# Hybrid decoder layer on one core: high products first in every unit, and a fifth place for up units

## Chip, core and metric

One core of a Trainium2 chip runs the whole layer. The time is the device time of one execution in microseconds; each kernel is run several times and the median counts. The profile shows one execution. Matrix products run on TensorE (PE), weight loads into it are shown as PEld; VectorE is DVE, ScalarE is ACT, GpSimd is POOL, and SyncE (SP) issues the loads and stores.

## The reference, cut to what matters

1024 prompt tokens and 8 x 4 sample tokens of width 1024 pass one layer in float32:

```python
h = rmsnorm(x, g_mix); proj = h @ w_in           # to a gated DeltaNet and a Conformer convolution
o, s_new = gated_delta_rule(q, k, v, g, beta, s0)
x = x + concat([o, cv]) @ w_out
h = rmsnorm(x, g_mlp)
x = x + square(relu(h @ w_up)) @ w_down          # 1024 -> 4096 -> 1024
gate = sigmoid(rmsnorm(x, g_ple) @ w_ple_gate)
x = x + (p_emb @ w_ple) * gate                   # and a last rmsnorm
```

Besides the two outputs the new DeltaNet states and convolution histories are returned.

## The kernel before, in words

**Products in three parts.** TensorE works in a rounded float32 form. To keep float32 accuracy every operand is split in a high part (the value rounded) and a remainder, and a product is the sum of three: high weights by high rows, high weights by low rows, low weights by high rows. The weights of a unit are loaded into `w_raw` (L732, SP), ScalarE rounds them to `w_hi` (`split_hi`, L968), VectorE subtracts to `w_lo` (`split_lo`, L1692), in place of `w_raw`. There are three slots of weights, so the load of a unit waits until the unit three places before it has been multiplied.

**Units.** `plan()` lists 258 jobs, called units here. A unit is one block of 128 columns of one weight matrix by all tokens of a segment. Segment 0 has 512 tokens (one piece of 512 columns), segment 1 has 544 (two pieces of 256 and 288). Most units have `kts` = 8 blocks of depth, hence 24 products in a piece; a down unit of segment 0 has 4 (12 products), a ple unit 2. The order of kinds is: input projection of both segments (ab, qkv, gb, ga, z), then `rest(0)`, then `rest(1)`; `rest` has 8 out units, then groups of up units and 8 down units each, then 8 pairs of gate and ple. `GROUPS` gives the up units in a group: 8 groups of 4 in segment 0, 4 groups of 8 in segment 1. A down unit sums over the up units of its group and is added to `xT`.

**Slots.** Every unit has two slots of the loop that all engines run in the same order. TensorE multiplies a unit in one go per slot (`multiply`, products at L1345): the two pieces of segment 1, or the two halves of the depth in segment 0. `TIMES` counts the slots in units of work, and `schedule()` puts side work (the samples, the chunked scan, the inverses, the norms, and the taps of the depthwise convolution on VectorE, L2046) at times of that count; the taps are spread so as to load VectorE evenly.

**Evictions.** A result lies in one of two PSUM banks, used in turn; the eviction frees it. For a unit of segment 0 it comes in the first slot of the next unit, and in VectorE's queue it stands right ahead of the `split_lo` of the unit after that one. Out and down units are added to `xT` (`take_rows`, L1730). An up unit goes: VectorE relu and scale (L1721), ScalarE square (L1045), ScalarE copy to `u_hi` (L1047), VectorE subtraction to `u_lo` (`finish_up`, L1808). After out units and after the last down units ScalarE writes `hh_hi` (L1036, L1057) and VectorE `hh_lo` (L1796); the operands of the out units are `op_hi` and `op_lo` (L2086).

**What a unit waits for.** At its first product TensorE waits for `w_lo` and for its bank. The first unit of each kind also waits, at the first product of each depth block, for the low rows of that block (`ready`). The products run block by block:

```python
for i in ks:
    ready(job, c, i)
    for n, (wt, x) in enumerate(((w_hi, rhs[0]), (w_hi, rhs[1]), (w_lo, rhs[0]))):
```

Of the kernel before, what the change touches and what calls it, by code (L numbers as in the profile page):

```python
# [7 lines left out]
F32 = mybir.dt.float32  # L8
# [5 lines left out]
P = 128  # L14
# [32 lines left out]
GROUPS = [[4] * 8, [8] * 4]  # L47

# [101 lines left out]
def schedule():  # L150
# [203 lines left out]
    for k in range(KT):  # L354
        put(done + 3 + 3 * k, "xr", 1, k)
# [88 lines left out]
def build(nc, a, o):  # L444
    ctx = ExitStack()
    with ctx:
# [3 lines left out]
        WR = CR + 18176 + 4 * H * HT  # L450
# [10 lines left out]
        def at(region, name, shape, dt=F32, off=None):  # L461

            if off is None:
# [28 lines left out]
        rate = at(CR, "rate", [P, H, HT])  # L492
        rn = at(CR, "rn", [P, NT + 1, 2 * H])
# [29 lines left out]
        uu = [[at(M0, f"u0_{n}", [P, GROUPS[0][0], TS[0]], F32R, off=49152 + 8192 * i) for i, n in enumerate(("hi", "lo"))],  # L523
              [at(MX, f"u1_{n}", [P, GROUPS[1][0], TS[1]], F32R, off=29696 + 17408 * i) for i, n in enumerate(("hi", "lo"))]]
# [36 lines left out]
        rateT = at(MX, "rateT", [H * HT, P])  # L561
        rates = at(MX, "rates", [P, C])
# [3 lines left out]
        Tbd = at(MX, "Tbd", [P, 2, H, P], off=12288)  # L566
# [152 lines left out]
        def _(sp):  # L719
# [243 lines left out]
        def _(act):  # L963
# [349 lines left out]
        def _(pe):  # L1313
            def ready(job, c, i):
# [3 lines left out]
                if job.kind == "ab" and i == 0:  # L1318
                    for done_rows in (x_hi, x_lo):
                        pe.wait_ge(done_rows, NT + 1 if s else HT)  # L1320
                elif job.kind == "out" and job.i == 0:
                    pe.wait_ge(op_lo, s * KT + i + 1)
                elif job.kind == "up" and job.i == 0:
                    pe.wait_ge(h_lo, lo_count(s, 0, k, c))
                elif job.kind == "gate" and job.i == 0:
                    pe.wait_ge(h_lo, lo_count(s, 1, k, c))
                elif job.kind == "down" and job.i == 0:
                    pe.wait_ge(u_lo, u_count(s, job.first + k, c))
                elif job.kind == "ple" and job.i == 0 and i == 0:
                    pe.wait_ge(b6, SIX[("pe", TILES[s][-1])] + 1)  # L1330

            def multiply(job, c, ks):
                s, m = job.s, job.m
                rhs = {"out": op, "up": hh, "gate": hh, "down": uu, "ple": pp}.get(job.kind, hm)[s]
# [5 lines left out]
                for i in ks:  # L1340
                    ready(job, c, i)
                    k = ORDER[i] if job.kind == "out" else i
                    end = i == job.kts - 1
                    for n, (wt, x) in enumerate(((w_hi, rhs[0]), (w_hi, rhs[1]), (w_lo, rhs[0]))):
                        last = nc.tensor.matmul(dst, wt[job.slot][:, k, 0:m], x[:, k, lo:hi], start=(i == 0 and n == 0),  # L1345
                                                stop=(end and n == 2))
                if ks[-1] == job.kts - 1:
# [325 lines left out]
            for h in range(SLOTS):  # L1673
                if h // 2 < len(JOBS):
                    job = JOBS[h // 2]
                    if job.n == 2:
                        multiply(job, h % 2, range(job.kts))
                    else:
                        multiply(job, 0, range(job.kts // 2) if h % 2 == 0 else range(job.kts // 2, job.kts))
# [6 lines left out]
        def _(dve):  # L1686
# [117 lines left out]
            def finish_up(job, c):  # L1804
                lo, hi = PIECES[job.s][c]
                i = job.i % GROUPS[job.s][0]
                dve.wait_ge(u_hi, u_count(job.s, job.i, c))
                nc.vector.tensor_tensor(uu[job.s][1][:, i, lo:hi], sg[:, lo:hi], uu[job.s][0][:, i, lo:hi].bitcast(F32),  # L1808
# [351 lines left out]
```

## Time and profile before

| | |
|---|---|
| Runs | 1666.9, 1668.41, 1675.49 us, median 1668.41 |
| The profiled execution's own time | 1667.82 us |
| Its span, first to last instruction | 1666.0 us |
| TensorE matmuls under way | 1535.3 us, 92% of the span |
| VectorE busy | 983.2 us, 59% |
| ScalarE busy | 710.6 us, 43% |
| GpSimd busy | 61.9 us, 4% |
| Mean granted TensorE clock | 0.967 |

The trace is read from TensorE outward: how long it stands idle, which instruction of which engine ended that idle time, and what that instruction itself had waited for or was queued behind. Matmuls are pipelined: their starts are recorded and their ends are modelled, so the start-to-start distance is the rate. A granted clock of 1.00 is the 2.4 GHz level, 0.50 the 1.2 GHz level.

### The profile page before, as it was taken

What the parts mean: (1) busy time and instruction counts of PE and PEld (TensorE: products, weight loads), DVE (VectorE), ACT (ScalarE), POOL (GpSimd) and SP (SyncE); (2) the same over time, 40 slices, a digit from 0 to 9 for tenths busy, and PEclk for the clock granted to TensorE, in tenths of its full rate; (3) what the DMA queues carried; (4) which work ended last, traced back from release to release, by engine and by line L of the source; (5) the groups of instructions that cost most, each with busy time, mean ns of one, the idle gap of its engine ahead of it and who ended that gap; (6) DMA issues with size and microseconds to landing.
All of it is one profiled execution on the core that took longest, in us unless ns stands there. A gap on an engine that the chain in (4) does not pass through costs nothing.

```text
span 1666.0 us, 27343 instructions
## 1 busy us (share of the span) xinstructions
PE 1535.3 (92%) x11338; PEld 1342.7 (81%) x11338; DVE 983.2 (59%) x1709; ACT 710.6 (43%) x1088; POOL 61.9 (4%) x84
## 2 busy tenths in 40 slices
PE   4898978999989899789999999899999999999987
PEld 2786777999877676566777877679899999999987
DVE  3664999787564747678964554656443434434553
ACT  5546534534546323435322244545541423224455
POOL 0000100000000030010000100000000000000000
PEclk9999989999899989999998999999999999999999
DMA  6254435233123333332331213423332323333322
GB/s 192 77 143 117 110 106 153 76 88 84 40 68 104 65 82 98 106 94 73 97 81 48 74 39 93 129 79 117 95 89 87 90 86 89 89 89 88 93 67 86
DMA packets 282512, 153.42 MB, mean 92 GB/s; under 512 B 37428, under 2 KB 273132, under 8 KB 282381
## 3 DMA queue, kind: packets, MB, share of 16 engines
q1 hardware_dynamic: 281367, 150.39, 31.6%
q8 instruction: 90, 1.47, 0.4%
q10 hardware_dynamic: 1022, 1.28, 0.3%
q14 instruction: 33, 0.27, 0.1%
HBM read 135.06 MB, written 17.00 MB: 91 GB/s over the span
## 4 chain that ended last, share of the span: by engine, by line
PE 70%; DVE 15%; ACT 7%; issue 4%; DMA 3%; ACTq 0%; POOL 0%; SPq 0%; DVEq 0%
PE ps L1345 58%; DVE of L2046 3%; PE ps L1488 2%; DVE w_lo L1692 2%; PE ps L1522 2%; PE ps L1516 2%; DVE Xp L1961 1%; DVE prod L1960 1%; DMA qt<-qkv_dram 1%; PE ps L1478 1%; ACT L972 1%; DVE yb L1721 1%; DVE u_lo L1808 1%; PE ps L1569 1%; DMA Lp<-lt_dram 1%
## 5 line engine op out<-in xcount | busy, mean ns | idle before, releaser
L1345 PE MATMUL ps<-hh_hi,w_hi 128*128 128x256 f32 (+1 forms) x960 | 317.9, 331 | 15.4 <-DVE w_lo L1692 9.6
L968 ACT ACTIVATE w_hi<-w_raw 128x1024 fp32r<-128x1024 f32 (+3 forms) x258 | 231.2, 899 | 214.9 <-DMA w_raw<-in_w_down 107.8
L1692 DVE TENSOR_TENSOR w_lo<-w_raw,w_hi 128x1024 fp32r<-128x1024 f32 (+3 forms) x258 | 266.5, 1033 | 86.9 <-ACT w_hi L968 86.0
L1345 PE MATMUL ps<-hh_lo,w_hi 128*128 128x256 f32 (+1 forms) x960 | 312.4, 325 | 0.0
L1345 PE MATMUL ps<-hh_hi,w_lo 128*128 128x256 f32 (+1 forms) x960 | 311.6, 325 | 0.0
L1345 PE MATMUL ps<-u_hi,w_hi 128*128 128x512 f32 (+2 forms) x768 | 256.5, 334 | 25.0 <-DVE u_lo L1808 18.7
L1345 PE MATMUL ps<-u_lo,w_hi 128*128 128x512 f32 (+2 forms) x768 | 249.3, 325 | 0.0
L1345 PE MATMUL ps<-u_hi,w_lo 128*128 128x512 f32 (+2 forms) x768 | 249.1, 324 | 0.0
L1345 PE MATMUL ps<-hm_hi,w_hi 128*128 128x512 f32 (+5 forms) x600 | 208.8, 348 | 13.4 <-DVE w_lo L1692 4.8
L1345 PEld LDWEIGHTS ps<-hh_hi,w_hi 128*128 128x128 f32 x960 | 182.8, 190 | 38.3 <-DVE w_lo L1692 18.7
L1345 PE MATMUL ps<-hm_lo,w_hi 128*128 128x512 f32 (+5 forms) x600 | 199.5, 332 | 0.0
L1345 PE MATMUL ps<-hm_hi,w_lo 128*128 128x512 f32 (+5 forms) x600 | 198.5, 331 | 0.0
L1345 PEld LDWEIGHTS ps<-hh_hi,w_lo 128*128 128x128 f32 x960 | 182.4, 190 | 14.0
L1345 PEld LDWEIGHTS ps<-hh_lo,w_hi 128*128 128x128 f32 x960 | 183.0, 191 | 12.9 <-issue 0.7
L1345 PEld LDWEIGHTS ps<-u_hi,w_hi 128*128 128x128 f32 x768 | 145.5, 189 | 44.4 <-DVE u_lo L1808 22.1
L2046 DVE SCALAR_TENSOR_TENSOR of<-gl,wdw,of 128x512 f32<-128x512 f32 x240 | 172.9, 763 | 1.1
L1730 DVE TENSOR_TENSOR xT<-xT,ps 128x512 f32<-128x512 f32 (+2 forms) x152 | 84.0, 553 | 131.4 <-PE ps L1345 131.0
L1345 PEld LDWEIGHTS ps<-u_hi,w_lo 128*128 128x128 f32 x768 | 145.3, 189 | 11.3
L1345 PEld LDWEIGHTS ps<-u_lo,w_hi 128*128 128x128 f32 x768 | 145.8, 190 | 10.2 <-issue 1.1
L1045 ACT ACTIVATE yb<-yb 128x256 f32<-128x256 f32 (+1 forms) x96 | 47.8, 498 | 230.6 <-DVE yb L1721 230.6
L1345 PEld LDWEIGHTS ps<-hm_hi,w_hi 128*128 128x128 f32 (+1 forms) x600 | 116.3, 194 | 29.2 <-issue 13.3
L1345 PEld LDWEIGHTS ps<-hm_lo,w_hi 128*128 128x128 f32 (+1 forms) x600 | 116.2, 194 | 11.6 <-issue 3.0
(286 smaller groups left out, 2035.5 us busy)
## 6 DMA issues: line engine op xcount, KB each, us to landing
w_raw<-in_w_up SPq DMA_DIRECT2D x64, 512.0 KB, 3.9
w_raw<-in_w_in SPq DMA_DIRECT2D x48, 512.0 KB, 4.1
w_raw<-in_w_down SPq DMA_DIRECT2D x64, 256.0 KB, 2.7
w_raw<-in_w_down SPq DMA_DIRECT2D x32, 512.0 KB, 4.0
w_raw<-in_w_out SPq DMA_DIRECT2D x16, 512.0 KB, 4.1
w_raw<-in_w_ple_gate SPq DMA_DIRECT2D x16, 512.0 KB, 4.1
qt<-qkv_dram SPq DMA_DIRECT2D x8, 768.0 KB, 5.9
xin<-in_x_prompt SPq DMA_DIRECT2D x8, 512.0 KB, 6.3
```

Of the source, the lines that this page charges most:

```text
L968: nc.scalar.activation(w_hi[job.slot][:, 0:job.kts, 0:job.m], w_raw[job.slot][:, 0:job.kts, 0:job.m], ACT.Copy).then_inc(w_hid, 1)
L972: ac.step(nc.scalar.activation(dst, src, ACT.Ln, **kw))
L1045: nc.scalar.activation(sg[:, lo:hi], yb[i % 2][:, lo:hi], ACT.Square).then_inc(u_sq, 1)
L1345: last = nc.tensor.matmul(dst, wt[job.slot][:, k, 0:m], x[:, k, lo:hi], start=(i == 0 and n == 0), stop=(end and n == 2))
L1478: last = nc.tensor.matmul(ps[:, 7, h * HD:(h + 1) * HD], T, Vb[:, t % HT, h * HD:(h + 1) * HD], start=True, stop=True)
L1488: last = nc.tensor.matmul(ps[r, bank + par, q * HD:(q + 1) * HD], src[rows, q, r], S[rows, q, :], start=(first or q == 0), stop=first, ski ...
L1516: last = nc.tensor.matmul(ps[par * HD:(par + 1) * HD, 2, q * HD:(q + 1) * HD], Kd[r, t % HT, h * HD:(h + 1) * HD], Vn[r, h * HD:(h + 1) * ...
L1522: last = nc.tensor.matmul(ps[r, 4 + par, q * HD:(q + 1) * HD], LQ[r, t % HT, par * PR + q, 0, :], Vn[r, h * HD:(h + 1) * HD], start=False, ...
L1569: last = nc.tensor.matmul(ps[rows, 2, q * 2 * NS:(q + 1) * 2 * NS].rearrange("p (w t) -> p w t", w=2)[:, :, cols], S0[rows, q, b, :], WQ[r ...
L1692: nc.vector.tensor_tensor(w_lo[job.slot][:, 0:job.kts, 0:job.m], w_raw[job.slot][:, 0:job.kts, 0:job.m], w_hi[job.slot][:, 0:job.kts, 0:jo ...
L1730: nc.vector.tensor_tensor(rows, rows, src, ALU.add).then_inc(freed(job, c), 1)
L2046: ins = nc.vector.scalar_tensor_tensor(out=rows, in0=gl[:, p, k:k + HALF], scalar=w, in1=rows, op0=ALU.mult, op1=ALU.add)
```

## The change

Three things change. Products of a unit are ordered high by high for all depth blocks first, then the two kinds with a remainder: high weights by low rows before low weights by high rows, in the first unit of a kind the other way round. TensorE waits for `w_hi` at the first product and for `w_lo` at the first product that uses it; the row waits are for high and low rows apart. In segment 0 a fifth place holds one more up unit: the first up unit of the next group runs ahead of the down units of this one (the last group has 3 up units left). ScalarE writes the square to `u_hi` first and then the plain square, in place of a square and a copy of it. Beside this some scratch moves to other addresses, and the loads of input rows 5 to 7 of segment 1 come after the last down unit of segment 0, since the fifth place lies in their memory.

```diff
+PLACES = [5, 8]
...
-        first = 0
+        first = made = 0
         for n in GROUPS[s]:
-            jobs.extend(Job("up", s, first + i) for i in range(n))
+            ready = min(first + PLACES[s], FF // P)
+            jobs.extend(Job("up", s, i) for i in range(made, ready))
             jobs.extend(Job("down", s, m, first, kts=n, last=first + n == FF // P) for m in range(KT))
-            first += n
+            first, made = first + n, ready
...
-        put(done + 3 + 3 * k, "xr", 1, k)
+        put(max(done + 3 + 3 * k, half("gate", 0, 0) + k - 4 if k > 4 else 0), "xr", 1, k)
...
+        u_fifth = [at(M0, "u0_hi4", [P, TS[0]], F32R, off=65536), at(MX, "u0_lo4", [P, TS[0]], F32R, off=12288)]
...
+        def u_rows(s, x, i):
+
+            k = i % PLACES[s]
+            return uu[s][x][:, k, :] if k < uu[s][x].shape[1] else u_fifth[x][:, :]
...
+                    if k > 4:
+                        sp.wait_ge(mm, last_unit("down", 0, KT - 1))
...
                 gone(act, job, c)
+                nc.scalar.activation(u_rows(s, 0, i)[:, lo:hi], yb[i % 2][:, lo:hi], ACT.Square).then_inc(u_hi, 1)
                 if i:
                     act.wait_ge(u_lo, u_count(s, i - 1, c))
                 nc.scalar.activation(sg[:, lo:hi], yb[i % 2][:, lo:hi], ACT.Square).then_inc(u_sq, 1)
-                act.wait_ge(u_sq, u_count(s, i, c))
-                nc.scalar.activation(uu[s][0][:, i % GROUPS[s][0], lo:hi], sg[:, lo:hi], ACT.Copy).then_inc(u_hi, 1)
...
+            def products(job):
...
+                first = (1, 0) if job.i == 0 else (0, 1)
+                rest = [(i, w, 1 - w) for w in first for i in range(job.kts)]
+                return [(i, 0, 0) for i in range(job.kts)] + rest
...
-                    for done_rows in (x_hi, x_lo):
-                        pe.wait_ge(done_rows, NT + 1 if s else HT)
+                    pe.wait_ge(x_lo if low else x_hi, NT + 1 if s else HT)
                 elif job.kind == "out" and job.i == 0:
-                    pe.wait_ge(op_lo, s * KT + i + 1)
+                    pe.wait_ge(op_lo if low else op_hi, s * KT + i + 1)
                 elif job.kind == "up" and job.i == 0:
-                    pe.wait_ge(h_lo, lo_count(s, 0, k, c))
+                    pe.wait_ge(h_lo if low else h_hi, lo_count(s, 0, k, c))
                 elif job.kind == "gate" and job.i == 0:
-                    pe.wait_ge(h_lo, lo_count(s, 1, k, c))
+                    pe.wait_ge(h_lo if low else h_hi, lo_count(s, 1, k, c))
                 elif job.kind == "down" and job.i == 0:
-                    pe.wait_ge(u_lo, u_count(s, job.first + k, c))
+                    pe.wait_ge(u_lo if low else u_hi, u_count(s, job.first + k, c))
...
-                if ks[0] == 0:
-                    pe.wait_ge(w_lod, job.j + 1)
+                remainder = min(n for n, (_, w, _) in enumerate(todo) if w)
+                if first == 0:
+                    pe.wait_ge(w_hid, job.j + 1)
                     wait(pe, pf[u % 2], u // 2)
...
+                for n in range(first, end):
+                    i, w, x = todo[n]
+                    if n == max(first, remainder):
+                        pe.wait_ge(w_lod, job.j + 1)
+                    if not w:
+                        ready(job, c, i, x)
                     k = ORDER[i] if job.kind == "out" else i
...
+                    last = nc.tensor.matmul(dst, weights[w][:, k, 0:m], rows[:, lo:hi], start=n == 0, stop=n == size - 1)
...
-                dve.wait_ge(u_hi, u_count(job.s, job.i, c))
+                dve.wait_ge(u_sq, u_count(job.s, job.i, c))
```

## Rows read from the trace of the kernel before

**Rows 1.** The page: busy time of engines, and the chain that ended last.
```profile
PE 1535.3 (92%) x11338; PEld 1342.7 (81%) x11338; DVE 983.2 (59%) x1709; ACT 710.6 (43%) x1088; POOL 61.9 (4%) x84
...
PE 70%; DVE 15%; ACT 7%; issue 4%; DMA 3%; ACTq 0%; POOL 0%; SPq 0%; DVEq 0%
```

**Rows 2.** Waits of TensorE: who for whom, us in total, times, longest us.
```profile
PE ps L1345 <- DVE w_lo L1692: 21.9, 22, 4.8
PE ps L1345 <- DVE u_lo L1808: 18.7, 8, 7.2
```

**Rows 3.** Timeline of TensorE (start us, us, instruction, idle before), first down unit, 702.
```profile
702.74 0.39 PE L1345 MATMUL ps<-u_hi,w_hi 128*128 128x512 f32 x1
702.97 0.39 PE L1345 MATMUL ps<-u_lo,w_hi 128*128 128x512 f32 x1
703.19 0.40 PE L1345 MATMUL ps<-u_hi,w_lo 128*128 128x512 f32 x1
...
710.82 0.80 PE L1345 MATMUL ps<-u_hi,w_hi 128*128 128x512 f32 x1 [7.23 <-DVE u_lo L1808]
```

**Rows 4.** Timeline of VectorE in the same stretch: eviction of up unit 11, its remainder.
```profile
708.04 0.68 DVE L1721 SCALAR_TENSOR_TENSOR yb<-ps,rs 128x512 f32<-128x512 f32 x1
...
710.08 0.69 DVE L1808 TENSOR_TENSOR u_lo<-yb,u_hi 128x512 fp32r<-128x512 f32 x1 [0.76 <-ACT u_hi L1047]
```

**Rows 5.** Waits of TensorE for u_lo, from 745 to 845, 845 to 975, 1015 to 1045.
```profile
PE ps L1345 <- DVE u_lo L1808: 3.6, 2, 2.2
...
PE ps L1345 <- DVE u_lo L1808: 3.3, 1, 3.3
...
PE ps L1345 <- DVE u_lo L1808: 0.8, 1, 0.8
```

**Rows 6.** Windows: stretch, length, busy PE PEld DVE ACT POOL, PEclk, DMA share, GB/s.
```profile
891.00:902.00 11.00, 11.00 (x74) 8.63 (x73) 1.73 (x3) 0.63 (x1) 0.61 (x1) 0.53 0.08 24
```

**Rows 7.** Waits of TensorE for w_lo, 1045 to 1066, to 1078, 1086 to 1128, to 1136.
```profile
PE ps L1345 <- DVE w_lo L1692: 2.3, 3, 1.4
...
PE ps L1345 <- DVE w_lo L1692: 3.5, 1, 3.5
...
PE ps L1345 <- DVE w_lo L1692: 3.3, 6, 0.6
...
PE ps L1345 <- DVE w_lo L1692: 1.2, 1, 1.2
```

**Rows 8.** Timeline of VectorE at 655: eviction, then the split of the next.
```profile
654.77 0.68 DVE L1730 TENSOR_TENSOR xT<-xT,ps 128x512 f32<-128x512 f32 x1
655.37 0.69 DVE L1692 TENSOR_TENSOR w_lo<-w_raw,w_hi 128x512 fp32r<-128x512 f32 x1
```

**Rows 9.** Timeline of all engines, last down units and gate unit 0.
```profile
1061.87 0.42 DVE L2091 TENSOR_TENSOR pp_lo<-ps,pp_hi 128x256 fp32r<-128x256 f32 x1 [1.04 <-ACT pp_hi L1254]
...
1065.34 0.50 PE L1345 MATMUL ps<-hh_hi,w_hi 128*128 128x512 f32 x1 [1.44 <-DVE w_lo L1692]
...
1067.25 0.72 ACT L1057 ACTIVATE hh_hi<-xT,vec 128x512 fp32r<-128x512 f32 x1 [1.45 <-DVE xT L1730]
```

**Rows 10.** Timeline of ScalarE and TensorE ahead of the first unit.
```profile
28.91 1.02 ACT L1091 ACTIVATE hm_hi<-ps 128x1024 fp32r<-128x1024 f32 x1 [1.31 <-PE ps L1375]
...
31.34 0.59 PE L1345 MATMUL ps<-hm_hi,w_hi 128*16 128x512 f32 x1 [2.46 <-DVE hm_lo L1855]
```

**Rows 11.** Timeline of TensorE in output unit 0.
```profile
484.66 0.51 PE L1345 MATMUL ps<-op_hi,w_hi 128*128 128x512 f32 x1 [3.10 <-DVE op_lo L2086]
```

**Rows 12.** Timeline of TensorE at z unit 2 of segment 1.
```profile
241.57 0.55 PE L1345 MATMUL ps<-hm_hi,w_hi 128*128 128x256 f32 x1 [4.67 <-ACT yb L1014]
```

**Rows 13.** Windows: VectorE alone (busy, PEclk, DMA), then all engines as in rows 6.
```profile
794.00:832.00 38.00, 35.14 (x67) 1.00 0.30 91
...
531.00:1134.00 603.00, 554.72 (x3621) 433.45 (x3619) 382.41 (x624) 234.07 (x340) 40.51 (x47) 0.96 0.30 84
...
1086.00:1128.00 42.00, 38.66 (x163) 29.82 (x163) 26.00 (x39) 20.35 (x32) 0.00 (x0) 1.00 0.31 92
```

More of the change, by code:

```diff
@@ L449, in build @@
         CR = base
-        WR = CR + 18176 + 4 * H * HT
+        WR = CR + 18176 + 4 * H * HT + 4 * C
         TR = WR + 3 * 8192
@@ L492, in build @@
         rate = at(CR, "rate", [P, H, HT])
+        rates = at(CR, "rates", [P, C])
         rn = at(CR, "rn", [P, NT + 1, 2 * H])
@@ L522, in build @@
                for i, n in enumerate(("hi", "lo"))] for s in range(2)]
-        uu = [[at(M0, f"u0_{n}", [P, GROUPS[0][0], TS[0]], F32R, off=49152 + 8192 * i) for i, n in enumerate(("hi", "lo"))],
-              [at(MX, f"u1_{n}", [P, GROUPS[1][0], TS[1]], F32R, off=29696 + 17408 * i) for i, n in enumerate(("hi", "lo"))]]
+        uu = [[at(M0, f"u0_{n}", [P, 4, TS[0]], F32R, off=49152 + 8192 * i) for i, n in enumerate(("hi", "lo"))],
+              [at(MX, f"u1_{n}", [P, PLACES[1], TS[1]], F32R, off=29696 + 17408 * i) for i, n in enumerate(("hi", "lo"))]]
+        u_fifth = [at(M0, "u0_hi4", [P, TS[0]], F32R, off=65536), at(MX, "u0_lo4", [P, TS[0]], F32R, off=12288)]
         op = [[at(MX, f"op{s}_{n}", [P, KT, TS[s]], F32R, off=32768 + 17408 * i)
@@ L560, in build @@
         trk = [at(MX, f"trk{n}", [P, H, C]) for n in range(2)]
-        rateT = at(MX, "rateT", [H * HT, P])
-        rates = at(MX, "rates", [P, C])
+        rateT = at(MX, "rateT", [H * HT, P], off=22528)
         cur[MX] = 30720
@@ L565, in build @@
         assert cur[MX] == 32768
-        Tbd = at(MX, "Tbd", [P, 2, H, P], off=12288)
+        Tbd = at(MX, "Tbd", [P, 2, H, P], off=14336)
         Lp = at(MX, "Lp", [P, C * C])
@@ L1313, in _, with ready @@
         def _(pe):
-            def ready(job, c, i):
+            def products(job):
+                first = (1, 0) if job.i == 0 else (0, 1)
+                rest = [(i, w, 1 - w) for w in first for i in range(job.kts)]
+                return [(i, 0, 0) for i in range(job.kts)] + rest
+            def ready(job, c, i, low):
                 s, n = job.s, len(PIECES[job.s])
@@ L1325, in ready @@
                 elif job.kind == "gate" and job.i == 0:
-                    pe.wait_ge(h_lo, lo_count(s, 1, k, c))
+                    pe.wait_ge(h_lo if low else h_hi, lo_count(s, 1, k, c))
                 elif job.kind == "down" and job.i == 0:
-                    pe.wait_ge(u_lo, u_count(s, job.first + k, c))
-                elif job.kind == "ple" and job.i == 0 and i == 0:
+                    pe.wait_ge(u_lo if low else u_hi, u_count(s, job.first + k, c))
+                elif job.kind == "ple" and job.i == 0 and i == 0 and not low:
@@ L1330, in ready, with multiply @@
                     pe.wait_ge(b6, SIX[("pe", TILES[s][-1])] + 1)
-            def multiply(job, c, ks):
+            def multiply(job, c, half=None):
                 s, m = job.s, job.m
-                rhs = {"out": op, "up": hh, "gate": hh, "down": uu, "ple": pp}.get(job.kind, hm)[s]
+                rhs = {"out": op, "up": hh, "gate": hh, "ple": pp}.get(job.kind, hm)[s]
+                weights = (w_hi[job.slot], w_lo[job.slot])
                 dst, lo, hi = out_of(job, c)
                 u = job.u + c
-                if ks[0] == 0:
-                    pe.wait_ge(w_lod, job.j + 1)
-                    wait(pe, pf[u % 2], u // 2)
-                for i in ks:
-                    ready(job, c, i)
-                    k = ORDER[i] if job.kind == "out" else i
[L1343 to L1347, printed above, removed]
+                todo = products(job)
+                size = len(todo)
+                first, end = {None: (0, size), 0: (0, size // 2), 1: (size // 2, size)}[half]
+                remainder = min(n for n, (_, w, _) in enumerate(todo) if w)
+                if first == 0:
+                    pe.wait_ge(w_hid, job.j + 1)
+                    wait(pe, pf[u % 2], u // 2)
+                for n in range(first, end):
[4 more added lines that the diff above has]
+                        ready(job, c, i, x)
+                    k = ORDER[i] if job.kind == "out" else i
+                    rows = u_rows(s, x, job.first + k) if job.kind == "down" else rhs[x][:, k, :]
+                    last = nc.tensor.matmul(dst, weights[w][:, k, 0:m], rows[:, lo:hi], start=n == 0, stop=n == size - 1)
+                if end == size:
@@ L1676, in _ @@
                     if job.n == 2:
-                        multiply(job, h % 2, range(job.kts))
+                        multiply(job, h % 2)
                     else:
-                        multiply(job, 0, range(job.kts // 2) if h % 2 == 0 else range(job.kts // 2, job.kts))
+                        multiply(job, 0, h % 2)
                 for stage in SIDE[h]:
```

3 lines of the change are left out of this document (1 added, 2 removed).

## Prediction

> **What bounds the kernel now.** I read the page first: TensorE has matmuls under way for 92% of the span, VectorE is busy for 59%, and the chain that ended last is 70% TensorE, 15% VectorE [rows 1]. So a microsecond that TensorE does not stand still is nearly a microsecond won, as long as VectorE's queue isn't what it then waits for. The second view is the waits of TensorE: the two largest at the product line L1345 are 22 waits for `w_lo` (21.9 us) and 8 for `u_lo` (18.7 us) [rows 2]. They are what this change aims at, 40.6 us, and the rest of the working asks of each what would be late next. The third view is the timeline around one wait. A product of 512 columns follows the last after 0.23 us, whether the weights stay (`u_hi,w_hi` to `u_lo,w_hi`) or change (to `w_lo`), and a product whose own wait is already met (702.74) starts as promptly. A wait costs its idle time and 0.17 us to start again: 703.19 to 710.82 is 7.63 us, of which 0.23 is the pitch and 7.23 the idle time [rows 3]. The first matmul behind a wait also lasts 0.50 us [rows 9], not 0.40 as at 703.19, and holds up the next by as much. So I count 0.28 us beside each wait's idle time.
>
> **Part 1, the fifth place.** It concerns units of segment 0 alone (segment 1 had 8 places for groups of 8). There each group ends with an up unit whose eviction is a chain: VectorE L1721, ScalarE L1045 and L1047, VectorE L1808, and the first down unit needs its `u_lo` at its tenth product, 2.1 us after it starts. With the next group's first up between (24 products, 5.5 us), that is due 5.5 us later. The waits of the first seven groups go: 18.7 less the last group's 0.8 (no up unit is left to put there) [rows 5] is 17.9, with 7 x 0.28 it is 19.9 us. One of them does not go whole. At 702 VectorE works off side work (a chunk's scaling) and empties up unit 11's bank only from 708.04 to 708.7 [rows 4]. There are two result banks used in turn, so the down unit behind the extra up unit (701.36 + 5.5 = 706.9) must wait for that bank: 1.9 us stay. **18.0 us.** In the last group the first down unit now needs `u_hi` at its fourth product, 0.7 us after it starts; the first ScalarE pass now writes `u_hi` itself, one pass earlier. I put that group at 0: about 1 us of wait for `u_hi` instead of 0.8 for `u_lo`.
>
> The two longest of these waits (7.2 and 3.3) had a second price: behind the 3.3 us wait TensorE ran at a granted clock of 0.53 from 891 to 902, which is the 1.2 GHz level for nearly all of it [rows 5, 6]. If all the work in those 11 us were twice as fast, 5.2 us would come back; if other gaps bring the level down anyway, nothing. I take **2.5 us** for both places together, about the middle, since small matmuls of side work fill much of that stretch.
>
> The extra unit moves two weight loads and their splits on SP, ScalarE and VectorE with it, in the same queues and in the same number. The side work (state scan, samples, inverses) is placed by time in units of work, so it keeps its time and gets another neighbour. I cost that at nothing.
>
> **Part 2, remainders last.** Every unit now waits for `w_hi` at its start and for `w_lo` only at its first product with it: 16 products later in an 8-deep unit (3.7 us), 8 later in a down unit of segment 0 (1.8 us), 8 later also in the first unit of each kind. All the idle times for `w_lo` but five are under 1.3 us, so the wait itself is gone. But in VectorE's queue the instruction just ahead of the split is the eviction that frees the bank the waiting unit writes: at 654.77 L1730, at 655.37 the split, both for the unit that starts at 656.11 [rows 8]. So the unit can start at most one split earlier (0.6 us in a down unit, 1.2 in a deep one) when VectorE has a backlog. By stretch:
> - Six waits at gate units of segment 0: 3.3 us idle [rows 7], each shorter than the 1.2 us split: whole, 3.3 + 6 x 0.28 = 5.0.
> - The first output unit of segment 1, 1.2 us [rows 7]: its pieces have 256 columns, so `w_lo` is due after 8 x 0.12 = 0.9 us: 1.0.
> - Ten waits in the up and down units: 21.9 - 4.8 - 2.3 - 3.5 - 3.3 - 1.2 = 6.8, with 2.8 for restarts 9.6; two of 1.5 and 1.6 us give one split each (less 1.7), one stands before side work that waits for GpSimd anyway (less 0.9): 7.0.
> - The 4.8 us wait of z unit 1 (segment 1) gives 0: 16 products could run early, but the unit behind it waits 4.7 us more for ScalarE's eviction, which VectorE's inverse work holds up [rows 12].
> - The last three of that kind ahead of the gates, 2.3 us, give 0. There the last down units run to a loop of 3.9 us between VectorE and ScalarE (L2091 idles 1.04 us in each round for ScalarE [rows 9]), and TensorE only gets ahead of it.
>
> Sum **13.0 us.**
>
> **What the new order costs.** A first unit of a kind now needs all its high rows after 7 products instead of its low rows after 21. For gate unit 0 the last `hh_hi` is written from 1067.25 to 1067.97 [rows 9]. TensorE stalls there, and 17 products are left: 1067.97 + 17 x 0.23 = 1071.9, where before the unit ended at 1071.0 (24 products from 1065.34). Everything to gate unit 1 then comes 0.9 later, except that this unit needn't wait for its 1.2 us split: **+0.3 us** is left of the 3.5 us wait [rows 7]. Up unit 0 pays the same way: **-0.4** (nothing to 0.9, the gate's value). Output unit 0 loses its 3.1 us wait for `op_lo` at the 19th product and finds another at the 23rd, with two products left instead of six at the low clock: **+1.2** [rows 11]. The very first unit waited 2.46 us for `hm_lo`; the matching `hm_hi` ends at 29.93, so it can start at 30.1 instead of 31.34: **+1.3** [rows 10].
>
> **Edits with no cost of their own.** ScalarE and VectorE have as many instructions as before, only the order of `u_hi` and the plain square turns round. Three loads of input rows move behind the last down unit; they are first needed in the output units of segment 1, some 60 us on. The waits added to TensorE are met ones elsewhere, at 0 [rows 3].
>
> **What is given back.** From 794 to 832 VectorE is busy 35.1 of 38 us [rows 13]. The changes of the stretch 745 to 845 (3.6 us for `u_lo` [rows 5] and about as much again) would load it to some 99%. I take off **2 us** (0 to 5).
>
> Sum: 18.0 + 2.5 + 13.0 + 0.3 - 0.4 + 1.2 + 1.3 - 2 = 33.9 us. The profiled execution took 1667.8 us, of which the span is 1666.0 and the rest lies around it unchanged, so 1633.9; the median of the runs is 0.6 above it: 1634.5.
>
> **A rule against the change.** At 702.74, 702.97 and 703.19 the pitch is 0.23 us whether or not the weights change, so their loads are hidden [rows 3]. The Trainium skill (TensorE: Matmul & The Clock Gate, Architectural detail) says that TensorE's queue pulls weight loads ahead of matmuls in flight. By that rule a wait amid a unit would stop this running ahead and cost a restart; the restart measured is 0.28 us, and it is paid only where the wait isn't met.
>
> **Rivals.**
> - **The banks and VectorE's queue take over.** With evictions in the same order, TensorE meets its bank where it met `w_lo` or `u_lo`. For it: rows 8 and 4. Against: the gates have 1.2 us of split between. Then Part 2's seven in the up and down units and half of Part 1's 18.0 go, and the clock's 2.5: 33.9 - 7.0 - 9.0 - 2.5 = 15.4 us won, 1652.
> - **The change doesn't do what it says**: `w_hi` and `u_hi` come as late as the remainders, because ScalarE (which waits for VectorE too) sets both. Only Part 1's short waits and the gates are won, 8 us or less: 1660 or above. Against: `w_lo` comes 0.6 to 1.2 us after `w_hi` by VectorE's own time alone.
> - **Slower: the clock.** Long waits become many short ones. Over 531 to 1134 the clock is 0.96 [rows 13]. If it fell to 0.84 there, a further 24% of 603 us would be at the low level and cost half of that, 72 us against 34 won: 1706. It decides at 34/(603 x 0.5) = 11% more time at the low level, a mean of 0.90. Against: from 1086 to 1128 six such waits leave it at 1.00 [rows 13]. The Trainium skill (same page, A second HAM failure mode) tells of a kernel whose clock swung through just such short pauses between groups; here no row shows it.
>
> **Chances.** Forecast (1624 to 1645) 0.68; banks and queue (to 1656) 0.2; doesn't do what it says 0.08, of which 0.02 just below 1660; slower 0.04. The range 1624 to 1654 leaves out the last two and the tail of the second. The bound of what can be told from no change is 0.5%, 8.3 us: faster 0.9, same 0.06, slower 0.04.
>
> **What would show it.** Waits of TensorE for `u_lo` fall from 8 to 1 or 2, those for `w_lo` to a few under 1 us; new waits for the evictions L1730 and L1721 sum to under 6 us; at gate unit 0 a new wait of about 2 us for `hh_hi` stands amid the unit; the clock from 885 to 905 is above 0.8. I am wrong if the waits for evictions sum to over 15 us, or if the side work's waits grow.

## Result: 9 us won of the 33 forecast

The changed kernel takes 1659.0 us (median of 9 runs, 1649.7 to 1661.5) against 1667.9 us: the ratio is 0.9934 (95% interval 0.9913 to 0.9954; the ratios in this document go by all runs of both kernels, not by the two medians). Forecast were 1634.5 us and a range of 1624 to 1654. The sign was right, the size was not: 8.9 us came of 33.4. The profiled execution took 1652.7 us, 15.2 under the one of before; why it looks better than the median is told below.

The page of the changed kernel, busy time and chain (compare [rows 1]):

```profile
PE 1534.3 (93%) x11338; PEld 1344.7 (81%) x11338; DVE 982.7 (60%) x1709; ACT 701.8 (43%) x1088; POOL 62.4 (4%) x84
...
PE 72%; DVE 12%; ACT 7%; issue 4%; DMA 3%; POOL 1%; ACTq 0%; SPq 0%; DVEq 0%; POOLq 0%
```

Below are the waits of TensorE from the first up unit of segment 0 to its last down unit, 528.9 to 1053.7, called the stretch from here on (who for whom, us in total, times, longest). L1372 is the product line, L1756 and L1747 are the evictions that were L1730 and L1721, L978 is `split_hi`:

```profile
PE ps L1458 <- DMA qt<-qkv_dram: 6.4, 1, 6.4
PE ps L1372 <- DVE xT L1756: 4.8, 3, 3.1
PE ps L1372 <- DVE yb L1747: 3.6, 3, 1.9
PE ps L1372 <- ACT w_hi L978: 3.0, 2, 2.5
PE ps L1637 <- ACT cn L1218: 2.2, 2, 1.2
...
PE ps L1372 <- ACT u_hi L1053: 0.8, 1, 0.8
```

Before, the same stretch (531 to 1065.4) had

```profile
PE ps L1345 <- DVE u_lo L1808: 18.7, 8, 7.2
PE ps L1345 <- DVE w_lo L1692: 9.1, 13, 1.6
```

Both are gone. In their place stand 13.6 us for banks, `w_hi` and a norm's `cn` (4.8 + 3.6 + 3.0 + 2.2) that were not there.

**What stood in TensorE's way.** VectorE around the longest new wait (start, us, instruction), and TensorE at its end:

```profile
651.01 0.69 DVE L1954 TENSOR_TENSOR Vb<-ps,beta 128x512 f32<-128x512 f32 x1
651.61 0.68 DVE L1954 TENSOR_TENSOR tk<-ps,egc 128x512 f32<-128x512 f32 x1
652.21 0.68 DVE L1954 TENSOR_TENSOR Kbe<-ps,scb 128x512 f32<-128x512 f32 x1
652.81 0.68 DVE L1954 TENSOR_TENSOR Kd<-ps,scb 128x512 f32<-128x512 f32 x1
653.41 0.68 DVE L1756 TENSOR_TENSOR xT<-xT,ps 128x512 f32<-128x512 f32 x1
...
654.23 1.94 PE L1372 MATMUL ps<-u_hi,w_hi 128*128 128x512 f32 x4 [3.10 <-DVE xT L1756]
```

This is the scaling of a chunk: ten instructions, and ahead of them a wait of 1.1 us for ScalarE that begins at 648.6. Until 653.41, 4.8 us in all, the eviction is queued behind. A down unit lasts 2.75 us (12 products at 0.229 us), so two banks can't cover it; an up unit lasts 5.5 us and can. ScalarE holds up `w_hi` in the same way at 777, with the inverse root of a norm (a logarithm and an exponential), two table loads among them (4.4 us from 773.14 to the end of `w_hi`):

```profile
773.14 1.28 ACT L1223 ACT_TABLE_LOAD   x1
774.44 0.69 ACT L1223 ACTIVATE cn<-ps,eps 128x512 f32<-128x512 f32 x1
775.14 1.28 ACT L1225 ACT_TABLE_LOAD   x1
776.44 0.63 ACT L1225 ACTIVATE cn<-cn 128x512 f32<-128x512 f32 x1
776.97 0.61 ACT L978 ACTIVATE w_hi<-w_raw 128x512 fp32r<-128x512 f32 x1
...
777.64 2.07 PE L1372 MATMUL ps<-u_hi,w_hi 128*128 128x512 f32 x4 [2.55 <-ACT w_hi L978]
```

### The profile page after: what moved, and what is told of

Same layout as the page of the kernel before. It is cut to its first block, busy times and chain, and to the rows that moved or that the text cites. A ratio compares the mean times of both kernels' runs of the same rounds, so it can differ in the third digit from the quotient of the medians.

```text
span 1650.9 us, 27248 instructions
## 1 busy us (share of the span) xinstructions
PE 1534.3 (93%) x11338; PEld 1344.7 (81%) x11338; DVE 982.7 (60%) x1709; ACT 701.8 (43%) x1088; POOL 62.4 (4%) x84
## 4 chain that ended last, share of the span: by engine, by line
PE 72%; DVE 12%; ACT 7%; issue 4%; DMA 3%; POOL 1%; ACTq 0%; SPq 0%; DVEq 0%; POOLq 0%
PE ps L1372 59%; PE ps L1514 3%; PE ps L1548 2%; DVE of L2071 2%; PE ps L1542 2%; DVE w_lo L1718 1%; DVE Xp L1986 1%; DMA qt<-qkv_dram 1%; DVE prod L1985 1%; PE ps L1504 1%; PE ps L1595 1%; ACT w_hi L978 1%; POOL VnM L952 1%; ACT L982 1%; DMA Lp<-lt_dram 1%
## 5 line engine op out<-in xcount | busy, mean ns | idle before, releaser
L978 ACT ACTIVATE w_hi<-w_raw 128x1024 fp32r<-128x1024 f32 (+3 forms) x258 | 231.7, 901 | 229.5 <-DMA w_raw<-in_w_down 114.2
L1372 PE MATMUL ps<-hh_hi,w_hi 128*128 128x256 f32 (+1 forms) x960 | 179.3, 329 | 11.6 <-DVE yb L1747 3.1
L1372 PE MATMUL ps<-hh_lo,w_hi 128*128 128x256 f32 (+1 forms) x960 | 178.9, 326 | 0.0
L1372 PE MATMUL ps<-hh_hi,w_lo 128*128 128x256 f32 (+1 forms) x960 | 173.3, 323 | 0.0
L1372 PEld LDWEIGHTS ps<-hh_hi,w_hi 128*128 128x128 f32 x960 | 145.9, 191 | 30.4 <-issue 11.1
L1372 PE MATMUL ps<-u_hi,w_hi 128*128 128x512 f32 (+2 forms) x768 | 154.8, 337 | 12.1 <-DVE xT L1756 4.8
L1756 DVE TENSOR_TENSOR xT<-xT,ps 128x512 f32<-128x512 f32 (+2 forms) x152 | 83.9, 552 | 129.0 <-PE ps L1372 128.7
L1372 PEld LDWEIGHTS ps<-hh_lo,w_hi 128*128 128x128 f32 x960 | 145.9, 190 | 14.5 <-issue 1.3
L1372 PEld LDWEIGHTS ps<-hh_hi,w_lo 128*128 128x128 f32 x960 | 145.6, 189 | 13.2
L1372 PE MATMUL ps<-u_lo,w_hi 128*128 128x512 f32 (+2 forms) x768 | 149.1, 328 | 0.0
L1372 PE MATMUL ps<-u_hi,w_lo 128*128 128x512 f32 (+2 forms) x768 | 144.8, 324 | 0.0
L1372 PEld LDWEIGHTS ps<-u_hi,w_hi 128*128 128x128 f32 x768 | 116.2, 192 | 29.3 <-issue 13.2
L1372 PE MATMUL ps<-hm_hi,w_hi 128*128 128x512 f32 (+5 forms) x600 | 121.8, 348 | 8.9 <-ACT yb L1024 6.6
L1372 PEld LDWEIGHTS ps<-u_lo,w_hi 128*128 128x128 f32 x768 | 118.1, 192 | 11.7 <-issue 0.2
L1372 PEld LDWEIGHTS ps<-u_hi,w_lo 128*128 128x128 f32 x768 | 117.1, 189 | 11.3
L1372 PEld LDWEIGHTS ps<-hm_hi,w_hi 128*128 128x128 f32 (+1 forms) x600 | 94.8, 196 | 27.1 <-issue 16.1
L1372 PE MATMUL ps<-hm_lo,w_hi 128*128 128x512 f32 (+5 forms) x600 | 114.1, 330 | 0.0
L1372 PE MATMUL ps<-hm_hi,w_lo 128*128 128x512 f32 (+5 forms) x600 | 111.1, 327 | 2.4 <-DVE w_lo L1718 2.4
L1747 DVE SCALAR_TENSOR_TENSOR yb<-ps,rs 128x256 f32<-128x256 f32 (+1 forms) x96 | 49.9, 521 | 101.1 <-PE ps L1372 87.1
```

The lines of the kernel that those rows point to most:

```text
L978: nc.scalar.activation(w_hi[job.slot][:, 0:job.kts, 0:job.m], w_raw[job.slot][:, 0:job.kts, 0:job.m], ACT.Copy).then_inc(w_hid, 1)
L1372: last = nc.tensor.matmul(dst, weights[w][:, k, 0:m], rows[:, lo:hi], start=n == 0, stop=n == size - 1)
L1747: nc.vector.scalar_tensor_tensor(out=yb[i % 2][:, lo:hi], in0=src, scalar=0.0, in1=rs[:, lo:hi], op0=ALU.max, op1=ALU.mult).then_inc(freed ...
L1756: nc.vector.tensor_tensor(rows, rows, src, ALU.add).then_inc(freed(job, c), 1)
```

## Where the time of the stretch goes

For the stretch I split TensorE's time, from start to start of its instructions, in four: idle time as the trace gives it, products at their pitch at 2.4 GHz (1536 times 0.229 us, 351.7 us, the same in all and not shown), what a product took beyond that, which is restart or the 1.2 GHz level ("over pitch"), and the time of the side work's matmuls ("side"). Worked out from the rows of each trace, us:

```
kernel (traces)            total   idle   over pitch   side
before                     534.3   40.3   29.9         112.3
fifth place alone, 1st     526.4   35.9   28.4         110.3
fifth place alone, 2nd     522.9   34.4   27.5         109.3
new order elsewhere (*)    530.3   34.4   32.7         111.5
new order here (*)         525.4   33.4   30.0         110.3
new order alone            535.4   38.1   35.3         110.3
both (the change), 1st     524.7   29.8   30.9         112.2
both, 2nd                  520.3   30.4   28.7         109.5
both, 3rd                  529.1   31.3   35.2         110.9
```

(*) The two halves of experiment 2, both with the fifth place.

The prediction has 25.1 us for this stretch (18.0 + 2.5 + 7.0 - 0.4 - 2): by its own terms some 18.4 us of idle time and 6.7 of restarts and clock. The three traces of the change have 9.6 us in the mean: 9.8 us less idle time, 1.7 us more over pitch, 1.4 us less side work. So a good half of the 15.5 us that are missing here (8.6) is idle time, new waits above all, and the rest is restarts and clock that didn't get less. Time over pitch varies between executions: "new order elsewhere" runs the same instructions in the stretch as "fifth place alone" and has 4 to 5 us more of it. Outside the stretch the prediction has 8.8 us and the three traces have 4.0 in the mean.

## Experiments

**1. Either part alone.** The fifth place with the old order of products and its waits, run twice:

```diff
-                rest = [(i, w, 1 - w) for w in first for i in range(job.kts)]
-                return [(i, 0, 0) for i in range(job.kts)] + rest
+                return [(i, w, x) for i in range(job.kts) for w, x in ((0, 0), (0, 1), (1, 0))]
...
+                    if n == 0:
+                        pe.wait_ge(w_lod, job.j + 1)
```

> The changed kernel with the old order of products (block by block, remainder weights waited for at the first product); the fifth place stays. The steps of the prediction: Part 1 brings 18.0 and the clock 2.5, less 2 for VectorE's load and 0.4 less for up unit 0 than the full change, so about 18 us under the kernel before (1650). Theory of the banks (down units are 2.75 us long, two banks cover one of them, and each block of side work that VectorE does ahead of an eviction now stops TensorE there): the waits for u_lo vanish, but waits for the evictions yb and xT of 5 to 9 us and the side work's own waits come in units 4 to 16 of the up units, and the gain is 2 to 8 us (1660 to 1666). Theory of the clock: the waits vanish and stay away, but the mean granted clock from up unit 0 to the last down unit falls by 0.02 or more.

Measured: 1660.7 us, ratio 0.9966 (0.995 to 0.9983), 12 runs; on another chip 1658.9, 0.9958 (0.9934 to 0.9981). The waits of the stretch:

```profile
PE ps L1370 <- DVE w_lo L1716: 16.5, 13, 3.1
...
PE ps L1635 <- ACT cn L1218: 2.2, 2, 1.2
...
PE ps L1370 <- DVE yb L1745: 1.0, 1, 1.0
PE ps L1370 <- DVE u_lo L1831: 0.8, 1, 0.8
```

The waits for `u_lo` fell by 17.9 us as forecast, and those for `w_lo` rose from 9.1 to 16.5. As I read it, the old wait for `u_lo` had given VectorE time to catch up; without it TensorE meets the same backlog one or two units later. My expectation had these waits under the names of evictions; they came as `w_lo`, the split right behind the eviction in the queue. The theory of the clock fails here: in the stretch the clock rose from 0.96 to 0.97 in both traces, and over whole runs its mean was 0.9669 (24 runs) against 0.9649 (72 runs of before).

The new order with four places:

```diff
-PLACES = [5, 8]
+PLACES = [4, 8]
```

> The changed kernel with four places for up units, so the order of units of the kernel before; only the order of products is new. The steps of the prediction: Part 2's 13.0 and 2.4 from the new order in the first units, 15.4 us under the kernel before (1652.5), of it 7.0 in up and down units of segment 0. Theory of the banks: the first units and the gates bring their 2.5 and 5, the up and down units next to nothing, so 6 to 9 us (1659 to 1662), with u_lo waits of 14 to 19 us as before, since the first down unit now needs u_lo two products earlier (its eighth product instead of its tenth). Theory of the clock: gain under 5 us, with a lower mean clock.

Measured: 1670.4 us, ratio 1.000 (0.9984 to 1.0015): nothing.

```profile
PE ps L1372 <- ACT u_hi L1053: 19.4, 8, 7.1
...
PE ps L1372 <- DVE xT L1756: 3.2, 2, 1.6
...
PE ps L1372 <- ACT w_hi L978: 0.7, 2, 0.5
```

The two longest `w_lo` waits, 1.6 and 1.5 us, are now waits of 1.6 and 1.5 us for the eviction ahead of the split. The split was 0.6 us of them, but TensorE also came that much earlier to its bank, since a short wait before was gone, and the eviction didn't: at the longer one it starts 10.70 us after the chunk's transposes in both kernels (644.07 to 654.77 before, 645.67 to 656.37 now). The waits for `u_lo` became waits for `u_hi`, since a first down unit needs its last high rows at the fourth product. The idle time of the stretch fell by 2.2 us, and 5.4 us more over pitch took it back. The mean clock was 0.9607 (12 runs).

**2. Which half of the new order pays.** With five places, the new order either everywhere but in the up and down units of segment 0, or in these alone, beside the kernels with none and all of it, on one chip:

```diff
+                if job.s == 0 and job.kind in ("up", "down"):
+                    return [(i, w, x) for i in range(job.kts) for w, x in ((0, 0), (0, 1), (1, 0))]
```

> Five places, the new order of products everywhere but in the up and down units of segment 0, which keep the old order and its waits. The forecast's terms for this part of the order: 5.0 at the gates, 1.0 and 0.3 at first units, 1.2 and 1.3 at output unit 0 and the first unit, 8.8 us under the kernel with five places and the old order (1660.7), so 1652. From the traces so far: gates 5.1, the rest next to nothing, so 1655 to 1656. If the new order lowers TensorE's clock and that is a matter of the order itself, the mean clock is under that of the old order (0.967) here too.

> The other half: five places, the new order in the up and down units of segment 0 alone. The forecast gives it 7.0 less 0.4 us, 1654. By the traces TensorE's waits in this part are 35.9 us with the old and 29.8 us with the new order, but what it gains lies in a part with slow-clock stretches: 2 to 6 us, 1655 to 1659.

> The kernel with five places and the old order once more, on the same chip as the two halves: 1660.7 before; 1659 to 1663, mean clock 0.966 to 0.968.

> The changed kernel once more beside its two halves. If the halves are independent, its gain over the old order with five places is the sum of theirs; 1656 to 1660, mean clock 0.963 to 0.965.

Measured: none of it 1658.9 us, 0.9958 (0.9934 to 0.9981); all but up and down units 1659.9, 0.9950 (0.9926 to 0.9975); these alone 1660.8, 0.9951 (0.9934 to 0.9968); all of it 1659.5, 0.9941 (0.9922 to 0.9960). Beside the fifth place the new order is worth 0.0017 of 1668, 3 us, inside the intervals (over 24 runs each the means are 1662.3 and 1658.2, the medians 1659.8 and 1659.2). Yet the gates' gain is in every trace: from gate unit 0 to output unit 0 of segment 1, 68.8 us before, 69.3 and 67.9 us with the fifth place and the old order, 64.2, 64.2 and 65.8 us with the new. In the stretch the new order has 4.7 us less idle time, and the stretch is no shorter: 524.7 us in the mean with either order. What goes with the loss is the clock. Its mean over the runs is 0.9669 (24 runs, old order), 0.9654 and 0.9664 with half of it, 0.9637 (24 runs) with all of it. Within the 24 runs of the changed kernel 0.01 of clock goes with 11 us, within the 24 of the old order with 13, so these 0.003 are some 4 us.

The traces show where. With the old order in the up and down units (three traces with the fifth place) the granted clock is 0.96 from 606 to 682 and 1.00 from 682 to 741; with the new order there (four traces) it is 0.91 to 0.93 and 0.97. The waits in front are alike: 3.1 us at 651 to 657 in all seven, then 1.8 us with the old order and 1.9 with the new at 711 to 716. From 705 to 725 the clock is 1.00 in the three and 0.91 in the four. So a wait of the same length is followed by the 1.2 GHz level with one order and not with the other.

**3. Is it the order itself that lowers the clock?** Four places, new order, all waits as before:

```diff
+                    if n == 0:
+                        pe.wait_ge(w_lod, job.j + 1)
+                    if not w and not x:
+                        ready(job, c, i, 0)
+                        ready(job, c, i, 1)
```

> Four places, the new order of products, but every wait where it was: for the remainder weights at a unit's first product, for both parts of the rows at the first product of each depth block. It asks what the order alone does to TensorE's clock: the new order with the new waits had a mean clock of 0.9607 over 12 runs against 0.9651 before, at 5 us per 0.0044. If the order of products lowers the clock, 0.960 to 0.962 again and 1672 to 1676, since nothing is won. If the places of the waits do, 0.965 and 1668 to 1671 (the u_lo waits of the down units come two to six products earlier, at no gain).

Measured: 1687.9 us, 1.0134 (1.0115 to 1.0152), clock 0.9614. I had the time wrong: with the low rows waited for in the first eight products, a first down unit needs `u_lo` at its fourth product instead of its tenth, and those waits grew by half (18.7 to 28.8 us).

```profile
PE ps L1372 <- DVE u_lo L1833: 28.8, 9, 7.7
```

So waits for high and low parts apart are what makes the new order bearable at all. The clock was as low as with the new waits, but the stretch had 12 us more idle time than before (51.8 against 40.3), so this decides nothing. **Why the new order goes with a lower clock stays open.**

**4. The same kernel again.**

> The changed kernel once more, word for word, for a second trace of it: its runs lie from 1649.7 to 1661.5, the one traced was 1652.67. If the spread is TensorE's clock, two traces whose times differ have the same waits and differ in the mean granted clock, in stretches at the 1.2 GHz level (a difference of 8 us needs 16 us more at that level); if it is DMA or queueing, the waits of TensorE differ. Median again 1659, 1656 to 1661.

Measured: 1658.0 us (6 runs), 0.9933 (0.9908 to 0.9957). Three traces of the changed kernel, span and clock:

```profile
core 0: 1650.9 us, clock 0.963
...
core 0: 1647.1 us, clock 0.968
...
core 0: 1659.1 us, clock 0.964
```

In the stretch their waits agree to 0.3 us for `xT`, `yb`, `u_hi` and `cn` and to 0.8 us for `w_hi`; the time over pitch is 30.9, 28.7 and 35.2 us. So the spread goes with the clock, as expected, though the mean over the span doesn't rank the first and third rightly. It also counts the first 31 us, where TensorE has matmuls under way for less than 9 us and the first trace has 0.92, the third 1.00. Which stretches fall to 1.2 GHz changes in part from run to run behind the same gaps: from 561 to 606 the three have 0.85, 0.92 and 0.86. The Trainium skill (TensorE: Matmul & The Clock Gate, What's actually happening) says that the moment of the clock's first rise varies between runs of one kernel, with where the start falls in the gate's own rhythm. The three traces show variation amid the kernel; where it comes from they don't show. The two first traces happened to be good ones: their mean gain is 17.0 us, the means of all runs differ by 10.4 (1668.6 over 81 runs and 1658.2 over 24).

**5. Load or blocks?** In both kernels the convolution taps of segment 1 work on 32 of 512 columns (the rest of those rows is left out):

```diff
+                    n = 32 if s else HALF
-                    ins = nc.vector.scalar_tensor_tensor(out=rows, in0=gl[:, p, k:k + HALF], ...
+                    ins = nc.vector.scalar_tensor_tensor(out=rows[:, 0:n], in0=gl[:, p, k:k + n], ...
```

> The kernel before with the taps of segment 1's depthwise convolution cut to 32 of 512 columns (all but the first tap of each part; the rest of these rows is left out of the computation), so VectorE's queue keeps its order and its waits and loses about 120 x 0.6 = 70 us of load between the first up unit and the last down unit. It is the base for the same cut in the changed kernel. If VectorE's load sets the waits for w_lo and u_lo, it is 8 us or more faster than the kernel before; if the chunk scaling and its chain do, the u_lo wait of 7.2 us at up unit 11 stays within 1.5 us and the gain is 2 to 6 us.

> The changed kernel with the same cut of taps. Theory of load (VectorE is too busy for the gain): against the same cut in the kernel before it gains 25 us or more, near the forecast 33.9, and its waits for the evictions xT and yb fall under 2 us. Theory of blocks (the four passes of a chunk's scaling and what they wait for stand ahead of an eviction in VectorE's queue, whatever the load around them): its waits for xT and yb keep over half of their 8.4 us and it gains 9 to 16 us against the same cut in the kernel before.

Measured: 1658.9 us, 0.9951 (0.9940 to 0.9963), and 1649.0 us, 0.9888 (0.9874 to 0.9903). VectorE is busy for 59 and 57 us less (983.2 to 924.1, 982.7 to 925.9; I had reckoned with 70). The change is worth 9.9 us with this load off, as much as with it. TensorE in the stretch, changed kernel with short taps:

```profile
PE ps L1372 <- DVE xT L1756: 4.3, 2, 3.4
...
PE ps L1372 <- DVE yb L1747: 0.5, 2, 0.3
```

The waits for `xT` behind the scaling stay, those for `yb` go: 4.8 of 8.4 us are left. So load is a part of these waits, but taking it off didn't bring the missing gain.

**6. The block itself.** The scaling cut in two, its last two wide passes behind the eviction, on top of the early loads of experiment 7:

```diff
+                passes = plan[:2] if HT <= t < NT else plan
...
         put(n, "sc", t)
+        if HT <= t < NT:
+            put(n + 1, "sd", t)
```

> The changed kernel with early qt loads, and the chunk scaling of segment 1 cut in two: the last two of its four wide passes (1.2 us at a pitch of 0.60 us) come one slot later, behind the eviction that the whole block stood ahead of. Theory of blocks: the two long waits for evictions in down units behind a scaling (3.1 us at up unit 8's group, 1.5 to 1.9 at up unit 12's) shrink by 1.2 us each, 2 to 4 us won (1642 to 1644). Rival (the block's start, set by the chain of squares and roots ahead of it, decides and not its length): waits and time as with the early loads alone, 1645.6 within 1.

Measured: 1644.3 us, 0.9864 (0.9848 to 0.9880), 1.3 us under its base, which can't be told from nothing. But the waits answer to the instruction: from 620 to 675 with the whole block, then cut,

```profile
PE ps L1372 <- DVE xT L1756: 3.3, 2, 3.1
```

```profile
PE ps L1374 <- DVE xT L1758: 2.1, 2, 1.9
```

The longest is shorter by 1.2 us, which is two passes at a pitch of 0.60 us. The one of 1.5 us in the next group (700 to 741) is now

```profile
PE ps L1374 <- DVE xT L1758: 0.3, 1, 0.3
```

That shows the block as the cause of these two waits, by dose. It shows nothing of the others: `yb` (3.8 us), `w_hi` (4.3 us) and `cn` (2.2 us) are as long with the cut as without; that blocks in the queues make them too is read from the timelines and not tested. (The stretch took 515.6 us against 518.9. In these two traces the last 530 us gave it back: 531.4 against 527.2, at a clock of 0.98 against 0.99.)

Then the chunk preparations moved between up units, in three versions:

```diff
-    for t in TILES[1][:HT]:
+    for t, up in zip(TILES[1][:HT], (9, 11, 13, 15)):
...
+        h = half("up", 0, up)
```

> The changed kernel with the preparation of segment 1's four chunks put at up units 9, 11, 13 and 15, so each chunk's scaling on VectorE stands between up units (5.5 us each) and none between down units (2.75 us each); the rest of the scan follows later by 11 units. Theory of blocks: the waits for the evictions xT and yb in segment 0's down units (8.4 us) go, with restarts 8 to 11 us under the changed kernel (1647 to 1651). Theory of load: VectorE has as much to do, so the waits turn up elsewhere, under 3 us gained. Both leave the 6.4 us wait for the second chunk's qt.

> The same placing with the two qt loads early. If the two causes are apart, their gains add: 8 to 11 and 12.4 us, together 1636 to 1640. If the early loads only worked because of the old placing, 1645.

> The kernel with the two early qt loads and the four chunk preparations between up units, now with the second and fourth of them half an up unit later, so that a chunk's pairs and the next chunk's transposes no longer share a slot: in the first version of this placing TensorE waited 10.6 us for QdT there. If that was the fault of that version alone, those 10.6 us go and with them this placing shows what the blocks cost: 1639 to 1645, at or under the old placing with early loads (1645.6). If blocks between down units are not what costs, it stays above 1648.

Measured: 1660.9 us, 0.9967 (0.9954 to 0.9980); with early loads 1659.6, 0.9952 (0.9940 to 0.9964); with early loads and the second and fourth half a unit later 1647.7, 0.9884 (0.9871 to 0.9898). The first two fail by my own doing: two chunks shared a slot and TensorE waited 10.6 us for `QdT`. The 6.4 us wait for segment 1's second `qt`, which I expected to stay, went with the placing itself, so the early loads had only the 4.4 us of segment 0 left to win. The third keeps 4.6 us of that. Its second and fourth scaling stand right ahead of the eviction of the last up unit before down units, with waits of 3.8 and 4.2 us; the first and third stand between up units and no bank is waited for there. The second:

```profile
PE ps L1372 <- DVE yb L1747: 8.0, 2, 4.2
...
693.69 0.68 DVE L1954 TENSOR_TENSOR Kd<-ps,scb 128x512 f32<-128x512 f32 x1
694.29 0.68 DVE L1747 SCALAR_TENSOR_TENSOR yb<-ps,rs 128x512 f32<-128x512 f32 x1
```

Moving these two blocks moved their waits. No placing here was better than the old one.

**7. A wait that the change doesn't touch.** The second chunk's columns are loaded in the slot in which TensorE transposes them. SyncE's issue, and TensorE:

```profile
666.27 0.46 SPq L770 DMA_DIRECT2D qt<-qkv_dram  x1
...
672.67 2.82 PE L1458 MATMUL ps<-c_ident,qt 128*128 128x128 f32 x12 [6.41 <-DMA qt<-qkv_dram]
```

```diff
-        put(h if t < 2 else loads, "qt", t)
+        put(h if t == 0 else loads, "qt", t)
...
-        put(h if t < HT + 2 else loads, "qt", t)
+        put(h if t == HT else loads, "qt", t)
```

> The changed kernel with two loads of qt (the second chunk of each segment) issued one placing earlier, in segment 0 three slots, in segment 1 ten slots ahead of now. TensorE stood still for them for 4.5 and 6.4 us in the trace of after. If idle time of TensorE here is worth its length, 10.9 us and 2 x 0.28 for restarts go: 11.5 us under the changed kernel (1647.5). If VectorE's queue or the side chain behind these loads is what bounds the stretch, or the clock gives it back, under 5 us.

> The kernel before with the two qt loads issued early, nothing else. Idle time for qt is 4.3 and 6.3 us there. If the loads are a cause of their own, it gains as much as the changed kernel did with them (12.4 us), 1655 to 1657; if they only paid because the fifth place had cleared what stands behind them, under 6 us.

Measured: on the changed kernel 1645.6 us, 0.9864 (0.9846 to 0.9881); on the kernel before 1654.4, 0.9920 (0.9907 to 0.9934). Two moved lines are worth some 13 us with or without the change, more than the change. The two waits were 10.9 us with the change, 11.5 with restarts: this idle time was worth its full length. The early loads with the change, whole or cut scaling, beat both kernels.

## Why the prediction was wrong, step by step

- **Part 1, the waits for `u_lo`: right.** 18.7 to 0.8 us in total, and the last group's wait is now one of 0.8 us for `u_hi`, as put there.
- **Part 1, what takes their place: wrong, by 11 us. This is the largest step that failed.** I worked out the next lateness at one place (702, 1.9 us) and priced the rest by saying that the side work "keeps its time and gets another neighbour. I cost that at nothing." But the neighbour is what counts. Alone the fifth place left 4.4 and 5.9 us less idle time in the stretch instead of 16.0: in the first, 7.4 us came back as `w_lo`, 2.2 as `cn`, 1.0 as `yb`, and the rest in small ones. At 702 itself the group's new waits are 1.9 and 1.5 us (forecast 1.9).
- **Part 2, ten waits in up and down units, 7.0: wrong.** Alone the new order took 2.2 us of idle time from the stretch. I had seen that the eviction stands ahead of the split and allowed one split for each long wait (what stays of 1.5 and 1.6 us is then 1.9 us and not 1.7, and their restarts stay too), but I added the gains up, and TensorE came earlier to evictions that didn't. Beside the fifth place it took 4.7 us (means 35.2 and 30.5), about the idle part of the 7.0, but out of waits that the fifth place had just made longer, and the stretch got no shorter by it.
- **Part 2, the gates, 5.0 and 0.3: nearly right.** From gate unit 0 to output unit 0 of segment 1 it is 4.1 us in the mean of three traces. The waits between gate units are gone. At gate unit 0 the new one was forecast at about 2 us, and ended at the last `hh_hi`. Behind it stands one that I had missed, for `w_hi`, where the 3.5 us for `w_lo` was:

```profile
1057.39 0.50 PE L1372 MATMUL ps<-hh_hi,w_hi 128*128 128x512 f32 x1 [1.91 <-ACT hh_hi L1066]
...
1066.08 2.28 PE L1372 MATMUL ps<-hh_hi,w_hi 128*128 128x512 f32 x7 [2.28 <-ACT w_hi L978]
```

- **Restarts and clock, 6.7 in the stretch: wrong, by some 8 us.** Over pitch were 29.9 us, and now 30.9, 28.7 and 35.2. The place I had named did improve, from 0.74 to 0.91:

```profile
885.00:905.00 20.00, 16.74 (x116) 13.13 (x116) 8.42 (x15) 2.79 (x5) 0.61 (x1) 0.74 0.18 47
...
885.00:905.00 20.00, 20.00 (x175) 16.49 (x173) 10.61 (x17) 2.94 (x6) 1.60 (x2) 0.91 0.19 53
```

  But stretches at 1.2 GHz appeared behind the new waits (606 to 682: 0.96 before, 0.93, 0.91 and 0.93 now), and why they do so with the new order alone is open. A clock term has to be taken over the whole kernel and several executions, not at the place where a wait goes.
- **Small terms.** First unit +1.3: its start came from 31.3 to 30.0. z unit 1: right, the wait behind it for ScalarE's eviction grew from 4.7 to 6.6 us [rows 12]. Up unit 0 -0.4: right. Output unit 0 +1.2: there at its end (9.5 us after its start instead of 10.6), gone in the side work behind it; to up unit 0 it is 56.4, 55.4 and 55.4 us instead of 54.8. First output unit of segment 1, +1.0: didn't come, its first product has a gap of 1.2 us in front as before.
- **Given back, 2:** the stretch from 794 on was the wrong place for it; the losses came where VectorE was less busy on average but had a block in its queue (for two of the waits this is shown, experiment 6).
- **Rivals.** "The banks and VectorE's queue take over" (1652) was the right mechanism for the idle time, with too little weight (a chance of 0.2), and was still 7 us too good: it had no loss to the clock in it. My sign of being wrong (waits for evictions over 15 us) was drawn for one name of the wait; they came under four, 13.6 us.

## To carry over

When a wait goes, list what the in-order queues of the other engines hold ahead of each instruction that the next two units need, and compare the longest block there with the time that the free banks cover: the average load doesn't tell it. Where one engine's lateness is set by another's last stop, the gains of single waits don't add up; do the sum along the queue, not along the table of waits. Look early for idle time behind a DMA that is issued just when it is needed: here it had no backlog behind it and paid in full.

## What the runs showed of the hardware

In four of the kernels here, with 12 or 24 runs each, the fastest and the slowest run lie 14 to 20 us apart. In the three traces of the changed kernel the waits agree to 0.8 us, and the stretches at 1.2 GHz do not. Kernels with the fifth place that differ only in the order of products and the waits that go with it had mean clocks of 0.9669 and 0.9637 over 24 runs each (standard errors 0.0008 and 0.0005). Behind a wait of 1.8 or 1.9 us the granted clock from 705 to 725 was 1.00 in three traces with the old order in these units and 0.91 in four with the new. I hadn't expected this and can't explain it.
